# Stick-breaking cumulative sums as two rounded products in place of one plain fp32 product

## What is computed

```python
z = jnp.einsum('bqhd,bkhd->bhqk', qb, kb).astype(jnp.float32) * scale
strict = s_idx < t_idx
log_fail = jnp.where(strict, jax.nn.log_sigmoid(-z), 0.0)
after = lax.cumsum(log_fail, axis=3, reverse=True) - log_fail
w = jnp.where(strict, jnp.exp(jax.nn.log_sigmoid(z) + after), 0.0)
outs.append(jnp.einsum('bhqk,bkhd->bqhd', w.astype(vb.dtype), vb))
```

## Time and profile before

| | |
|---|---|
| median of 3 runs | 883.03 us (882.95 to 885.43) |
| the profiled execution's own time | 882.74 us |
| its span, first to last instruction | 880.8 us |
| mean granted TensorE clock | 0.996 |
| PE busy | 853.7 us (97%), 7200 instructions |
| DVE busy | 540.8 us (61%), 592 instructions |
| ACT busy | 394.7 us (45%), 461 instructions |
| POOL busy | 6.8 us (1%), 8 instructions |
| DMA | 140.61 MB, mean 160 GB/s |

### The profile page before, as it was taken

How to read it: one execution, slowest core, us unless ns; L and a number is a source line. 1 busy time by engine, 2 the same in 40 slices (tenths; PEclk the granted TensorE clock), 3 DMA queues, 4 the chain that set the end, 5 groups by cost and what they waited for, 6 DMA issues and landing times.

```text
span 880.8 us, 16424 instructions
## 1 busy us (share of the span) xinstructions
PE 853.7 (97%) x7200; PEld 787.0 (89%) x7200; DVE 540.8 (61%) x592; ACT 394.7 (45%) x461; POOL 6.8 (1%) x8
## 2 busy tenths in 40 slices
PE   6999999999999999999999999999998999999997
PEld 6999889998988999999998989988887899999996
DVE  4898745445777765555556655477644665555664
ACT  6453331337356543343446344455535543333332
POOL 0000020000000000000000000000000000000000
PEclk9999999999999999999999999999999999999999
DMA  9745512231474646555653744426433365555541
GB/s 317 245 144 170 166 50 79 68 99 50 142 265 144 219 164 202 182 188 183 199 191 96 240 144 144 144 96 235 144 106 116 119 212 187 183 186 189 188 142 48
DMA packets 96715, 140.61 MB, mean 160 GB/s; under 512 B 2449, under 2 KB 79377, under 8 KB 96657
## 3 DMA queue, kind: packets, MB, share of 16 engines
q1 hardware_dynamic: 96368, 139.62, 48.7%
q10 hardware_dynamic: 288, 0.13, 0.1%
HBM read 138.69 MB, written 1.05 MB: 159 GB/s over the span
## 4 chain that ended last, share of the span: by engine, by line
PE 92%; DVE 3%; ACT 2%; issue 1%; DMA 1%; POOL 0%; POOLq 0%; SPq 0%; DVEq 0%; ACTq 0%
PE PS L393 90%; DVE wlo L1431 1%; PE PS L468 1%; DMA raw<-in_w_in_dram 1%; ACT st L1033 1%; ACT xh L1033 1%; ACT whi L1033 1%; DVE xl L1461 0%; PE PS L548 0%; PE PS L879 0%; POOLq L97 0%; DVE xn L1950 0%; POOL TT L1022 0%; POOL TT L1026 0%; DVE st L1622 0%
## 5 line engine op out<-in xcount | busy, mean ns | idle before, releaser
L1431 DVE TENSOR_TENSOR wlo<-raw,whi 128x2048 fp32r<-128x2048 f32 x125 | 285.7, 2291 | 153.5 <-ACT whi L1033 153.4
L393 PE MATMUL PS<-xh,whi 128*128 128x256 f32 x1136 | 326.8, 288 | 7.9 <-DVE xl L1461 7.7
L393 PE MATMUL PS<-xl,whi 128*128 128x256 f32 x1136 | 323.0, 284 | 0.0
L393 PE MATMUL PS<-xh,wlo 128*128 128x256 f32 x1136 | 323.0, 284 | 0.0
L1033 ACT ACTIVATE whi<-raw 128x2048 fp32r<-128x2048 f32 (+1 forms) x127 | 240.3, 1896 | 177.0 <-PE PS L393 163.8
L393 PEld LDWEIGHTS PS<-xh,whi 128*128 128x128 f32 x1136 | 219.5, 193 | 14.3 <-issue 8.4
L393 PEld LDWEIGHTS PS<-xl,whi 128*128 128x128 f32 x1136 | 219.6, 193 | 0.9
L393 PEld LDWEIGHTS PS<-xh,wlo 128*128 128x128 f32 x1136 | 219.5, 193 | 0.0
L393 PE MATMUL PS<-whi,fh 128*128 128x512 f32 x216 | 84.3, 391 | 0.0
L393 PE MATMUL PS<-wlo,fh 128*128 128x512 f32 x216 | 84.3, 390 | 0.0
L393 PE MATMUL PS<-whi,fl 128*128 128x512 f32 x216 | 84.0, 389 | 0.0
(11 more groups left out here) (303 smaller groups left out, 1056.5 us busy)
## 6 DMA issues: line engine op xcount, KB each, us to landing
raw<-in_w_in_dram SPq DMA_DIRECT2D x32, 1024.0 KB, 5.3
raw<-in_w_up_dram SPq DMA_DIRECT2D x16, 1024.0 KB, 5.4
raw<-in_w_down_dram SPq DMA_DIRECT2D x16, 1024.0 KB, 5.0
raw<-in_w_ffn_gate_dram SPq DMA_DIRECT2D x11, 1024.0 KB, 5.3
raw<-in_w_ffn_up_dram SPq DMA_DIRECT2D x11, 1024.0 KB, 5.4
raw<-in_w_ffn_down_dram SPq DMA_DIRECT2D x11, 1024.0 KB, 5.0
raw<-in_w_kv_mem_dram SPq DMA_DIRECT2D x8, 1024.0 KB, 5.4
raw<-in_w_o_dram SPq DMA_DIRECT2D x4, 1024.0 KB, 7.7
```

Of the source, the lines that this page charges most:

```text
L393: return nc.tensor.matmul(o, l, r, start=start, stop=stop, **kw)
L1431: V.tensor_tensor(wlo[u % RING][:], raw[u % RING][:], whi[u % RING][:].bitcast(f32), ALU.subtract) \
```

## The change

The masked rows `st2` are split into a rounded part `lfh` (ACT) and the rest `lfl` (DVE), both of type float32r. `lfh` lies in the memory of `st3`, `lfl` over `st2` itself. Triangle and ones are rounded once, at the first pair, into `tri_r` and `ones_r`. PE forms each sum twice, with `lfh` and with `lfl`, into the same banks. The semaphore that DVE signals after the mask is now `sb_masked`; `sb_lf` comes after the subtraction.

```diff
--- before.py
+++ after.py
@@ -141,6 +141,11 @@
         st2 = at("st2", W + 85, [P, 2, 384])
         st3 = at("st3", W + 88, [P, 2, 384])
         st4 = at("st4", W + 91, [P, 2, 384])
+
+        lfh = at("lfh", W + 88, [P, 2, 384], f32r)
+        lfl = at("lfl", W + 85, [P, 2, 384], f32r)
+        tri_r = at("tri_r", 82.5, [P, P], f32r)
+        ones_r = at("ones_r", 83, [P, P], f32r)
         lora = at("lora", W + 94, [P, HW])
         gup = at("gup", W + 96, [P, HW])
         stg = [at(f"stg{i}", XR + 2.0625 * i, [P, 2, SEQ + 1]) for i in range(2)]
@@ -674,10 +679,14 @@
                 gate_unit(2 * p_)
 
                 pe.wait_ge(sem("sb_lf"), p_ + 1)
-                for e in range(2):
-                    mm(PS[:, (4 + e) * 512:(4 + e) * 512 + 384], C("tri"), st2[:, e, :], False, False, skip_group_check=True)
-                for e in range(2):
-                    last = mm(PS[:, (4 + e) * 512 + P:(4 + e) * 512 + SEQ], C("ones"), st2[:, e, SEQ:384], False, True, skip_group_check=True)
+                pe.wait_ge(sem("sums_rounded"), 1)
+                for part in (lfh, lfl):
+                    for e in range(2):
+                        mm(PS[:, (4 + e) * 512:(4 + e) * 512 + 384], tri_r[:], part[:, e, :], False, False, skip_group_check=True)
+                for part in (lfh, lfl):
+                    for e in range(2):
+                        last = mm(PS[:, (4 + e) * 512 + P:(4 + e) * 512 + SEQ], ones_r[:], part[:, e, SEQ:384], False, part is lfl,
+                                  skip_group_check=True)
                 last.then_inc(sem("sb_arg"), 1)
                 gate_unit(2 * p_ + 1)
 
@@ -1170,6 +1179,13 @@
                 link(A_(st1[:], PS[:, 4 * 512:6 * 512].rearrange("p (e n) -> p e n", e=2)[:, :, 0:384], ACT.Abs))
                 link(A_(st1[:], st1[:], ACT.Exp, scale=-1.0))
                 A_(st1[:], st1[:], ACT.Ln, bias=1.0).then_inc(sem("sb_ln"), 1)
+                if p_ == 0:
+                    A_(tri_r[:], C("tri"), ACT.Copy)
+                    A_(ones_r[:], C("ones"), ACT.Copy).then_inc(sem("sums_rounded"), 1)
+                act.wait_ge(sem("sb_masked"), p_ + 1)
+                if p_:
+                    act.wait_ge(sem("sb_w"), p_)
+                A_(lfh[:], st2[:], ACT.Copy).then_inc(sem("sb_hi"), 1)
                 if p_ == 3:
                     bank_pair(WT, "chunk_mm", 1, "chunk_ready")
                 if p_:
@@ -1620,7 +1636,10 @@
                 if p_:
                     dve.wait_ge(sem("sb_arg"), p_)
                 link(V.scalar_tensor_tensor(out=st2[:], in0=z, scalar=0.0, in1=st1[:], op0=ALU.max, op1=ALU.add))
-                V.tensor_tensor(st2[:], st2[:], M("sb_neg").unsqueeze(1).broadcast_to([P, 2, 384]), ALU.mult).then_inc(sem("sb_lf"), 1)
+                V.tensor_tensor(st2[:], st2[:], M("sb_neg").unsqueeze(1).broadcast_to([P, 2, 384]), ALU.mult).then_inc(sem("sb_masked"), 1)
+                dve.wait_ge(sem("sb_hi"), p_ + 1)
+                dve.wait_ge(sem("sb_masked"), p_ + 1)
+                V.tensor_tensor(lfl[:], st2[:], lfh[:].bitcast(f32), ALU.subtract).then_inc(sem("sb_lf"), 1)
                 if p_ == 1:
                     pair_out(AK, "strict", 3)
                 gate_unit(2 * p_)
```

## The result

| | before | after |
|---|---|---|
| median | 883.12 us | **898.73 us** (898.03 to 899.62, 4 runs) |
| ratio | | 1.0171, 95% interval 1.0151 to 1.0192 |
| profiled execution | 882.74 us | 899.41 us |
| span | 880.8 us | 897.6 us |
| mean granted clock | 0.996 | 0.981 |

The kernel is 15.6 us slower. I had forecast 7.3 us, with 892.7 as the end of the range. The direction was right; the forecast had less than half of the size.

A forecast was written before the change was run, and what follows sets the result against it. PE's chain of waits was taken to bound the kernel, with 92% of the span. Delays of 8.92 us less 1.62 saved gave +7.3 us: 890.0 profiled, 890.3 us forecast as median, range 886.8 to 892.7.

The forecast's parts named there:

- PE's four waits: Forecast waits on PE: about 2.6 us for XT, 3.5 for AK, 2.8 for Gm, 2.4 for WT.
- `whi` 2.9 us after Ln at pair 2: Profile sign on ACT: whi of pair 2 starts 2.9 us after Ln's end instead of right behind.
- the 0.96 that I took: A pair's eight new sum products on PE were to take 0.96 us, against 1.84 before.
- my upper value for slow small products: Eight sums at 0.12 us for each 128-column product would make 1.17 us a pair.
- 1.62: Total saving in us from faster sums on PE: 0.25 at pair 1, 0.8 at pair 2, 0.57 at pair 3.
- The delays' 8.9: Late PE inputs over four pairs: 1.87 + 1.87 + 2.77 + 2.41 = 8.92 us.
- The forecast's own sign of being wrong: On PE, a pair's eight sums taking over 1.2 us would show the forecast wrong.
- the clock falls: Rival: PE's two longest new gaps lower its clock, adding 4.3 us, for 894.6 us; chance 6%.
- the last sign in the prediction: A granted clock under 1.00 in the stage would show the forecast wrong.
- evidence at 1.64 us: Before, PE never stood longer than 1.64 us in this stage and the clock stayed at 1.00.
- the two waits that were new: Gaps on PE of 2.8 and 2.4 us, called the two longest new ones, were to lower the clock.
- the last stretch of the program: Last 10.8 us, PE busy for 4.6: mean clock 0.80, read as 4.3 us at the lower level, costing 2.2.

The follow-up runs named there:

- e11_late_split_early_ak: The change with lfh copied and lfl subtracted behind what PE waits for, and AK evacuated early on DVE; 880.16 us, ratio 0.9974.
- e1: The change with ACT copying lfh behind whi or WT and DVE subtracting behind XT or Gm; 881.6 us, ratio 0.9986.
- e13: The kernel before, plain sums, with only AK evacuated early on DVE; 882.50 us, ratio 0.9997.
- e2: The change, with PE running unread products in the four gaps before XT, AK, Gm and WT; 891.37 us, ratio 1.0086.
- e4: The kernel before, with three idle DVE operations behind the mask of pair 2, a gap before the join; 891.12 us, ratio 1.0089.
- e7: The kernel before, with two idle DVE operations behind the mask of pair 2, a gap before the join; 889.90 us, ratio 1.0078.
- e6: The kernel before, with one idle DVE operation behind the mask of pair 2, a gap before the join; 887.40 us, ratio 1.0052.
- e12: The kernel before, with PE waiting for a late st3 behind the sums of pair 2, ahead of a gate unit; 886.70 us, ratio 1.0042.
- e3_plain_sums: The change with the split kept, but sums as plain fp32 products of lfl only; 901.23 us, ratio 1.0189.
- e5: The change with lfh and lfl made behind what PE waits for, and XT and AK evacuated early; 882.37 us, ratio 0.9993.

## Why the prediction was wrong

**Right: what bounds the kernel, and where the change would hurt.** PE's four waits had the lengths that the steps gave, each within 0.1 us. Each wait ended as named, on `XT`, `AK`, `Gm` and `WT`. `lfh` took 0.85 and `lfl` 0.96 us as assumed, and rounding triangle and ones was hidden (0.29 and 0.30 us). (One number of the forecast doesn't fit its own steps: `whi` 2.9 us after Ln at pair 2, where 163.56 - 160.80 is 2.8. Measured, it is 2.8.)

**Nearly right: the sums.** From the profile of e11_late_split_early_ak, where the clock is up, pair 2:

```profile
168.64 0.62 PE L398 MATMUL PS<-lfh,tri_r 128*128 128x384 f32 x2
169.09 0.52 PE L398 MATMUL PS<-lfl,tri_r 128*128 128x384 f32 x2
169.46 0.34 PE L398 MATMUL PS<-lfh,ones_r 128*128 128x128 f32 x2
169.63 0.39 PE L398 MATMUL PS<-lfl,ones_r 128*128 128x128 f32 x2
169.85 0.33 PE L398 MATMUL PS<-xh,whi 128*128 128x256 f32 x1
```

1.21 us instead of the 0.96 that I took; my upper value for slow small products was 1.17. The 128-column products start about 0.09 to 0.11 us apart, not 0.067; the 81 ns of the Trainium skill (TensorE: Matmul & The Clock Gate, "Back-to-back issue gap") are nearer to that than mine. At pair 2 the saving is 0.55 us, not 0.8 (before, 170.11 to 171.87). All pairs together save 1.1 us and not 1.62: that is what e1 has less than before from mask to scan, and e11 less than e13. The delays' 8.9 less 1.1 is 7.8, and with the gaps filled 7.7 were measured. The forecast's own sign of being wrong, sums of over 1.2 us, is just met, but it explains only 0.5 of the 8.4 us between forecast and result.

**Wrong: the sum has no term for the clock.** The forecast is 8.92 - 1.62, waits less savings, all at the full clock; the lower clock was left to the rival "the clock falls", with 6% and 4.3 us. Measured, the clock cost 7.4 us (e2 against the change), as much as the whole sum. It is this step that put the time outside the range, and the last sign in the prediction, a granted clock under 1.00 in the stage, says so: over 98 to 210 us it is 0.91.

Three things failed in the step. First, evidence at 1.64 us was taken to speak for 2.7 us; gaps of 1.8, 2.1 and 3.1 us before the join all had the clock down behind them, and one of 1.1 us did in some runs, to go by their times. Second, the rival counted only the two waits that were new (2.8 and 2.4 us), though by the same sum PE stands 3.5 us for `AK` and 2.6 for `XT`; a fall followed the one for `XT`. Third, I priced a fall by the last stretch of the program and not by what follows the gap. Behind the gap for `Gm` the clock stayed down from 171.3 us until 184.9, through the join, the sums and most of a gate unit. In that state a gate product starts every 0.21 us instead of 0.12:

```profile
181.04 0.41 PE L398 MATMUL PS<-xl,whi 128*128 128x256 f32 x1
181.25 0.41 PE L398 MATMUL PS<-xh,wlo 128*128 128x256 f32 x1
```

And there was a further fall, in the scan, that I hadn't thought of at all. It cost 2.7 us in the profiled execution of the change. e1_late_split has it too, without a new gap in the stage, and what brings it is not shown.

The rule that I had put behind this rival, that idle gaps between bursts of matmuls let the gate fall back (the Trainium skill, TensorE: Matmul & The Clock Gate, "HAM oscillation"), points the right way in e1, e2, e4 and e7, and by the runs' times in e6. The gap for `AK` in the change (3.54 us) and the one in e12 (3.04 us) had no fall behind them. It was the one rule that spoke against the forecast, and it deserved more than 6%.

## What to carry to other kernels

On a kernel whose matrix engine never rests, a new hand-over between two helper engines is to be placed behind everything on both queues that the matrix engine will ask for next. Here the same operations cost 15.6 us in one place and nothing in another. Price a new gap of 1 us or more in TensorE at its own length plus 0 to 5 us of lower clock, and take the upper end as a likely case and not a remote one, above all where small products follow; count the whole gap, not only what is new in it. Then check by filling the gap with products that nobody reads.

## What the runs showed that I had not expected

- **A short gap costs all or nothing.** 1.1 us before the join gave either 0 or 3 to 5 us on top, in runs of one kernel. 2.1 and 3.1 us gave 4.8 and 5.0 by the medians, 3.3 and 4.8 within the stage of the profiled executions.
- **The place of a gap counts as much as its length.** 3.08 us before the join cost 8.1 us, 3.04 us before a gate unit 3.7.
- **A gap of 3.54 us left the clock at 1.00** in the profiled execution of the change, and one of 3.4 us at the same place did not in e3_plain_sums. The gap of 2.23 us ahead of the sums in e5 left it at 1.00 too, and so did the old 1.64 us for `AK` before.
- **DVE seems to have stood still while POOL worked**: the mask, with two inputs in SBUF, took 2.21 us beside a POOL operation that ran until 105.54 + 2.15 = 107.69 us, and ended 0.80 us after it, where it takes 0.96 alone. The Trainium skill (SBUF — State Buffer, "SBUF: two separate sides") says that a DVE operation with two SBUF inputs and a GpSimd operation that reads SBUF lock each other out for the whole instruction. The rows agree.
